# One TensorE-bound block kernel: rope, SiLU and softplus moved into the first projection, the delta rule's norms and turns into the local attention

## The reference, cut to what matters

```python
h = _rms_norm(x, g_mix_pre[l])
proj = h @ w_in[l]
aq, ak, av, dqkv, dgate, dalpha, dbeta = jnp.split(proj, IN_SPLITS, axis=-1)
aq = _rope(aq.reshape(b, s, ATTN_HEADS, ATTN_HEAD_DIM), positions)        # 8 heads of 64
ak = _rope(ak.reshape(b, s, ATTN_KV_HEADS, ATTN_HEAD_DIM), positions)     # 2 heads of 64
attn_o = _window_attention(aq, ak, av, attn_sink[l])                      # band of 128 each way
dn_o = _gated_deltanet(dqkv, dgate, dalpha, dbeta, conv_w[l], a_log[l], dt_bias[l], g_dn_out[l])
...
# in _gated_deltanet
conv = jax.nn.silu(conv.astype(jnp.float32))                              # 1536 channels, 5 taps
q = _l2norm(q) * (DN_HEAD_K ** -0.5)                                      # 4 heads of 128
k = _l2norm(k)
g = -jnp.exp(a_log) * jax.nn.softplus(a + dt_bias)
beta = jax.nn.sigmoid(bt)
# in each chunk, both directions
g = jnp.cumsum(g, axis=-1)
```

## Time and profile before

| what | value |
|---|---|
| median of 3 runs | 3808.03 us (3807.52 to 3812.46) |
| the profiled execution, first to last instruction (its span) | 3802.9 us |
| PE busy | 3621.9 us, 95% |
| DVE busy | 1925.5 us, 51% |
| ACT busy | 1436.0 us, 38% |
| `w_in` until the `rope_tables` barrier | to about 161 us |
| `rope_tables` and `rope` | about 161 to 184.8 us |
| `window` | 184.8 to 231.4 us |
| `delta_prep` | 231.4 to 267.2 us |

### The profile page before, as it was taken

How to read it: one execution, slowest core, us unless ns; L and a number is a source line. 1 busy time by engine, 2 the same in 40 slices (tenths; PEclk the granted TensorE clock), 3 DMA queues, 4 the chain that set the end, 5 groups by cost and what they waited for, 6 DMA issues and landing times.

```text
span 3802.9 us, 50067 instructions
## 1 busy us (share of the span) xinstructions
PE 3621.9 (95%) x19324; PEld 2946.7 (77%) x19324; DVE 1925.5 (51%) x3902; ACT 1436.0 (38%) x2538; POOL 107.4 (3%) x183
## 2 busy tenths in 40 slices
PE   7989989999999999999999989999899998889999
PEld 6779976788887888777777768888788886678887
DVE  5856746555455545555555544333433345764333
ACT  3251132432233222465556543223332234863222
POOL 0000001010001000000000000000000000000000
PEclk9999999999998999999999989999999999999999
DMA  6200036235543554211111212232223221012222
GB/s 243 95 1 1 1 128 226 89 121 176 187 147 125 192 177 146 81 67 51 51 51 50 73 54 89 89 111 89 90 83 117 72 75 45 2 45 89 87 91 78
DMA packets 47161, 359.77 MB, mean 95 GB/s; under 512 B 5217, under 2 KB 5601, under 8 KB 28129
## 3 DMA queue, kind: packets, MB, share of 16 engines
q1 hardware_dynamic: 23472, 269.31, 19.4%
q0 software_dynamic: 23472, 87.50, 6.9%
HBM read 354.69 MB, written 2.10 MB: 94 GB/s over the span
## 4 chain that ended last, share of the span: by engine, by line
PE 84%; DVE 8%; issue 3%; ACT 3%; DVEq 1%; DMA 0%; PEld 0%; ACTq 0%; PEldq 0%; POOL 0%; SPq 0%; POOLq 0%
PE bank L843 22%; PE bank L848 21%; PE bank L849 21%; PE bank L1679 5%; PE bank L2012 1%; PE bank L2029 1%; PE bank L2000 1%; PE bank L984 1%; PE bank L2485 1%; PE bank L2452 1%; DVE w_lo_sb L1280 1%; PE bank L1988 1%; PE bank L805 1%; PE bank L823 1%; PE bank L2474 1%
## 5 line engine op out<-in xcount | busy, mean ns | idle before, releaser
L843 PE MATMUL bank<-x_hi_sb,w_hi_sb 128*128 128x512 f32 x2936 | 1174.4, 400 | 59.6 <-DVE x_lo_sb L1422 15.7
L849 PE MATMUL bank<-x_hi_sb,w_lo_sb 128*128 128x512 f32 x2936 | 1151.4, 392 | 0.0
L848 PE MATMUL bank<-x_lo_sb,w_hi_sb 128*128 128x512 f32 x2936 | 1151.1, 392 | 0.0
L843 PEld LDWEIGHTS bank<-x_hi_sb,w_hi_sb 128*128 128x128 f32 x2936 | 555.5, 189 | 211.5 <-issue 66.1
L1103 ACT ACTIVATE w_hi_sb<-slab_sb 128x1024 fp32r<-128x1024 f32 (+2 forms) x555 | 507.1, 937 | 499.4 <-PE bank L843 312.0
L1280 DVE TENSOR_TENSOR w_lo_sb<-slab_sb,w_hi_sb 128x1024 fp32r<-128x1024 f32 (+2 forms) x555 | 580.8, 1078 | 187.4 <-ACT w_hi_sb L1103 172.2
L849 PEld LDWEIGHTS bank<-x_hi_sb,w_lo_sb 128*128 128x128 f32 x2936 | 555.0, 189 | 119.6
L848 PEld LDWEIGHTS bank<-x_lo_sb,w_hi_sb 128*128 128x128 f32 x2936 | 556.1, 189 | 109.2
L1446 DVE TENSOR_TENSOR hid_sb<-silu_gate_sb,bank 128x512 f32<-128x512 f32 x110 | 75.6, 687 | 602.1 <-PE bank L849 602.1
L843 PE MATMUL bank<-hid_hi_sb,w_hi_sb 128*128 128x512 f32 x880 | 342.8, 390 | 0.0
L849 PE MATMUL bank<-hid_hi_sb,w_lo_sb 128*128 128x512 f32 x880 | 342.6, 389 | 0.0
(11 more groups left out here) (361 smaller groups left out, 3742.4 us busy)
## 6 DMA issues: line engine op xcount, KB each, us to landing
slab_sb<-weights SPq DMA_DIRECT2D x79, 2048.0 KB, 7.9
keep_sb<-ada POOLq DMA_DIRECT2D x133, 512.0 KB, 4.5
slab_sb<-weights SPq DMA_DIRECT2D x44, 1536.0 KB, 6.5
slab_sb<-weights SPq DMA_DIRECT2D x20, 1280.0 KB, 6.0
tables_sb<-ada POOLq DMA_DIRECT2D x14, 512.0 KB, 6.2
work_sb<-ada POOLq DMA_DIRECT2D x13, 512.0 KB, 8.0
h_sb<-x SPq DMA_DIRECT2D x4, 512.0 KB, 6.7
out<-h_sb SPq DMA_DIRECT2D x8, 256.0 KB, 2.0
```

The costliest lines, as they stand in the source:

```text
L843: mm = pe.matmul(out, w_hi[p][:, w], hi, start=first, stop=False)
L848: pe.matmul(out, w_hi[p][:, w], lo, start=False, stop=False)
L849: return pe.matmul(out, w_lo[p][:, w], hi, start=False, stop=last)
```

## The change

Three barriers leave each engine's program, those that end `rope_tables`, `rope` and `delta_prep`. The one that ends `w_in` now stands behind the work of the first two, and the one that ends `window` behind that of the third.

- In `w_in`, the last slab is re-ordered so that the token-major part comes before the last two gate tiles. PE swaps tiles 0 and 1 after tile 18, tiles 2 and 3 after tile 19, tiles 4 and 5 after the token-major part. DVE ropes them in place. The angles are computed between weight parts in the first five steps; ACT takes the sines in step 7 and one SiLU tile per step from step 8 on. The softplus runs while PE is in the last tiles; PE makes the decay sums last.
- In `w_in`, 14 pieces of the modulation remain of 20. Six go to the first feed-forward layer: three pieces instead of two after each hidden tile of its first and last slabs.
- In `window`, `attend` calls a function `aside(i)` at the end of each iteration on each engine. PE: the sums of squares in i = 0 and 1, two spreads in each of i = 4 to 7, one tile's transposes in each of i = 3 and 8 to 14. ACT: four squares ahead of the loop, the roots in i = 2 with two table loads, copies of the transposes, three exponentials in i = 7. DVE: four squares and the decays ahead of the loop, the inversion in i = 3, two multiplications in each of i = 5 to 8.
- The dummy matmuls of `rope_tables`, `rope` and `delta_prep` go.

```diff
-ADA_TURNS = (20, 35, 105)
-ADA_EARLY = 52
+ADA_TURNS = (14, 35, 111)
+ADA_EARLY = 58
...
+                if aside is not None:
+                    aside(i)
...
+        def dve_rope_tile(e, j):
+            s = e.take(e.A, e.acc)
+            x, tmp = b1_qk[:, j, :], (b1_tmp[:, 3, :], b1_cv[0][:, 0:S])[j % 2]
+            dve.tensor_tensor(tmp, bank[s][:, :], b1_sin, ALU.mult).then_inc(e.A.free[s], 1)
+            e.link(dve.tensor_tensor(x, x, b1_cos, ALU.mult), dve_step)
+            dve.tensor_tensor(x, x, tmp, ALU.add)
...
+        DN_TILES = (4, 5, 6, 7, 0, 1, 2, 3)
+        DN_SPREADS = (4, 5, 6, 7)
+        DN_TURNS = (9, 10, 11, 12, 3, 8, 13, 14)
+        def pe_delta_ahead(e, i):
+            if i < 2:
+                if i == 0:
+                    e.norms = e.give(e.A, e.acc)
+                for j in DN_TILES[4 * i:4 * i + 4]:
+                    if j >= 4:
+                        pe.wait_ge(squared, e.nth(squared))
+                    else:
+                        pe.wait_ge(queries_squared, j + 1)
+                    for b in range(NB):
+                        at = j * NB + b
+                        mm = pe.matmul(e.A.bank[e.norms][:, at:at + 1], sq[:, j, b * P:(b + 1) * P], ones1, start=True,
+                                       stop=True)
...
+            if i in DN_SPREADS:
+                if i == DN_SPREADS[0]:
+                    pe.wait_ge(inverted, e.nth(inverted))
...
+            if i in DN_TURNS:
+                x = DN_TURNS.index(i)
+                if x < 4:
+                    pe.wait_ge(normed, e.nth(normed))
+                t = e.give(tp, e.tp)
+                for b in range(NB):
+                    mm = pe.transpose(turn_bank[t][:, b * P:(b + 1) * P], b1_qkv[:, 4 + x, b * P:(b + 1) * P], ident)
+                mm.then_inc(tp.full[t], 1)
+        def act_delta_ahead(e, i):
+            if i == 2:
+                act_root(e, 32, 1.0)
+                act_table(e, ACT.Exp)
...
             pe_parts_opening(e, x_hi, x_lo)
-            for _ in range(4):
+            for _ in range(3):
                 pe_parts(e, PARTS, KT, x_hi, x_lo, by_tile=True)
+            pe_parts(e, PARTS, KT, x_hi, x_lo, by_tile=True, between={2: swap(0), 3: swap(2)})
             e.slab.next()
+            pe_token_parts(e, 2, 2 * P, 2 * P)
+            pe_swap(e, b1_qk, 2, False, 4)
             for _ in range(2):
                 pe_tile_parts(e)
-            pe_token_parts(e, 2, 2 * P, 2 * P)
             pe_settle(e)
+            pe_decay_sums(e)
             e.stage_end("w_in")
-            pe_stay_busy(e, 40)
-            e.stage_end("rope_tables")
-            pe_swap(e, b1_qk, 6, wait=False)
-            pe_stay_busy(e, 20)
-            e.stage_end("rope")
-            attend(e, window_units(), 1, None)
+            attend(e, window_units(), 1, None, aside=lambda i: pe_delta_ahead(e, i))
...
+            dve_w_lo(e, 2, D)
+            dve.wait_ge(sines_ready, 1)
+            dve_rope_tile(e, 0)
+            dve_rope_tile(e, 1)
+            dve_w_lo(e, 3, D)
+            e.acc.pos += 1
+            dve_rope_tile(e, 2)
+            dve_rope_tile(e, 3)
+            dve_ada(e, 4)
             for b in range(NB):
                 s = e.take(e.A, e.acc)
                 dve.tensor_copy(b1_vtm[:, b, :], bank[s][:, 0:144]).then_inc(e.A.free[s], 1)
+            dve_decay_rates(e)
+            dve_rope_tile(e, 4)
+            dve_rope_tile(e, 5)
+            dve_decays(e)
+            dve_ada(e, 4)
...
                 if at in ("first", "mid", "last"):
-                    dve_ada(e, 2)
+                    dve_ada(e, 2 if at == "mid" else 3)
```

More of the change, by code:

```diff
@@ L540, in two_blocks @@
         b1_tmp = cut(work, 11848, 4, S)
-        b1_cos, b1_sin = b1_tmp[:, 0, :], b1_tmp[:, 1, :]
+        b1_cos, b1_sin = b1_tmp[:, 2, :], root_rows[:, :].bitcast(F32)
         P_SB = [cut(work, 11848 + 768 * i, 768) for i in range(3)]
-        PT = [cut(work, 14152 + 768 * i, 768) for i in range(2)]
+        PT = [cut(work, 768 * i, 768) for i in range(2)]
         m_col = [small[:, 160 + 24 * i:164 + 24 * i] for i in range(2)]
@@ L828, in pe_token_major, with pe_swap @@
                     between[b]()
-        def pe_swap(e, x, tiles, wait=True):
+        def pe_swap(e, x, tiles, wait=True, first=0):
             pe = e.eng
-            for j in range(tiles):
+            for j in range(first, first + tiles):
                 if wait:
@@ new lines, in dve_delta_squares @@
+        def dve_delta_squares(e):
+            dve = e.eng
+            for j in range(4):
+                dve.tensor_tensor(sq[:, j, :], b1_qkv[:, j, :], b1_qkv[:, j, :], ALU.mult).then_inc(queries_squared, 1)
+            e.tp.pos -= 1
+            t = e.take(tp, e.tp)
+            dve.tensor_copy(dn_s["G"], turn_bank[t][:, 0:32].rearrange("p (b x) -> p b x", b=NB))
+            e.link(dve.tensor_copy(dn_s["gl"], turn_bank[t][:, 32:64].rearrange("p (b x) -> p b x", b=NB)), dve_step)
+            dve.tensor_tensor(dn_s["diff"], dn_s["gl"], dn_s["G"], ALU.subtract).then_inc(dn["to_exp"], 1)
+            dve.drain().then_inc(tp.free[t], 1)
@@ new lines, in dve_delta_ahead @@
+        def dve_delta_ahead(e, i):
+            dve = e.eng
+            if i == 3:
+                dve_invert(e, 32, float(P) ** -0.5, 16)
+            if i - 1 in DN_SPREADS:
+                at = 2 * (i - 1 - DN_SPREADS[0])
+                for j in DN_TILES[at:at + 2]:
+                    s = e.take(e.S, e.sc)
+                    x = dve.tensor_tensor(b1_qkv[:, j, :], b1_qkv[:, j, :], e.S.bank[s][:, :], ALU.mult)
+                    x.then_inc(e.S.free[s], 1)
+                if j >= 4:
+                    dve.drain().then_inc(normed, 2)
+            if i == 9:
+                dve.wait_ge(dn["dec"], e.nth(dn["dec"]))
+                dve.tensor_tensor(dn_s["bG"], dn_s["beta"], dn_s["eG"], ALU.mult)
@@ L1656, in pe_delta @@
[L1656 to L1662, removed]
@@ L1820, in dve_delta @@
             dve.reciprocal(dn_s["beta"], dn_s["eb"])
[L1821 to L1835 removed]
+        def dve_delta(e):
+            dve = e.eng
+            tt = dve.tensor_tensor
+            for w in ways:
+                dve.memset(w.S, 0.0)
             full = [P, DH, P]
```

210 lines of the change are left out of this document (112 added, 98 removed).

## The result

The changed kernel takes **3788.5 us** (median of 4 runs, 3786.8 to 3789.9) against 3807.8 beside it: ratio 0.9945, 95% interval 0.9934 to 0.9957. That is 19.3 us faster. The forecast was 26.6 us, 3781, with a range of 3771 to 3796. The profiled execution took 3789.9 us, 1.9 over its span of 3788.0. Its span is 14.9 us under that of before. The missing 4 us lie in the executions: with 1.9 us around its span the profiled one of before took 3804.8, 3 us under its median, and the one here is 1.4 over its own. So the traces can explain 14.9 us, a little over half of the forecast.

The account below looks back on a forecast made before the run. PE, busy for 95% of the span, was taken to bound the kernel. Gains of 13.0 us (`w_in`) and 14.8 (35.8 of `delta_prep` less 21.0 window growth), less 1.2 (feed-forward), gave 26.6 us: 3781 us, range 3771 to 3796.

Parts of the forecast that it names:

- the 75 at which I would have called the account wrong: Stated sign of failure: the prediction is wrong if the window takes over 75 us; 67.7 was forecast.
- End of `w_in`: Last projection record to first score matmul: 24.4 us go, 11.4 us of PE work and waits replace them, 13.0 us gained.
- Head of the window: Window, i = 0 to 2: 64 records of sums at the low clock cost 11.6 us; i = 2 ends 8.9 us later.
- ACT's root: Window, i = 2 and 3: ACT's table load, root and load back take 3.1 us and PE waits; +3.8 us.
- Spreads, i = 4 to 7: Window: spreads add 1.83 us to each iteration, PE sets the pace at 4.1 instead of 2.45 us; +6.9 us.
- back at 1.00 by i = 4: Sign in the window: the clock is 0.50 over the sums and back at full by the fifth iteration.
- Turns: Window, i = 8 to 14: a transpose costs PE 0.46 and ACT 0.5 us; seven times 0.2, +1.4 us.
- First feed-forward layer: Second slab: PE's wait for DVE's weight part grows, as three modulation pieces precede it instead of two; 1.2 us lost.
- easy window: Rival: the window grows by only 12 us, as engines idle at its head and tail; 3772 us, chance 0.19.
- lockstep: Rival: each engine's new work stands where the next one waits; the window grows 35 us; 3795 us, chance 0.14.
- Low clock through the window: Rival: PE stays at 1.2 GHz through the window, about 105 us instead of 67.7; 3818 us, slower, chance 0.04.
- The loads of the modulation: Rival: 8.1 us reloads set the end of `w_in`, PE waits 2.4 us more before swap 4; 3788 us, chance 0.09.

Follow-up runs that it names:

- Run 6: Changed kernel with only VectorE's modulation pieces moved (three ahead of the value copies, two at the first feed-forward tile): median 3787.4 us, ratio 0.9943.
- run 2: Changed kernel with the squares and the 64 sums moved into the projection, a tile's sums between two projection tiles: median 3788.3 us, ratio 0.9939.
- run 3: As run 2, with the root and its inversion also moved into the projection stage: median 3774.9 us, ratio 0.9915.
- run 5: Changed kernel with the eight turns moved to units with four blocks and one behind the last: median 3787.5 us, ratio 0.9944.
- run 1: Changed kernel with squares, sums, root, spreads and turns done in one block behind the attention loop, not within it: median 3789.7 us, ratio 0.9954.
- run 11: The changed kernel once more, unedited, on the chip of run 9: median 3792.1 us, ratio 0.9949.
- run 4: As run 3, with VectorE's count of the score ring advanced by one, on the other chip: median 3780.8 us, ratio 0.9924.
- run 7: Run 4's kernel with 37 unused matmuls (8.5 us) added in the first feed-forward layer: median 3788.3 us, single runs 3778.4 to 3791.9.
- run 9: Changed kernel with sums, root and inversion in the projection, turns at four-block units, modulation pieces spread, decay sums at the stage's end: median 3771.7 us, ratio 0.9894.
- run 8: Changed kernel with sums, root and inversion in the projection, turns and modulation pieces moved, decay sums between the two gate tiles: median 3776.0 us, ratio 0.9911.

## Why the prediction held, point by point

The range held with room, and the change moved the time as forecast, but the parts that were off nearly all cost time. By the profiled executions the gain is 14.9 us of 26.6. The other 4.4 us of the measured 19.3 come from how the two profiled executions lie to their medians, which is luck. Without them the time would be 3793, still inside. One reading of mine was wrong as well: the 5.1 us "around the span" are 1.9 in every execution, and the rest is that the profiled one of before was 3 us faster than its median. The window took 74.4 us, just under the 75 at which I would have called the account wrong.

- **End of `w_in`**: forecast 13.0, measured 12.2. The modulation piece and its reload came out within 0.3 us. PE waited 1.35 instead of 2.1, and 0.57 instead of 0.8 in the token-major part; the decay sums with the gap behind them took 3.7 instead of 3.1, since the clock fell in them. About 1.2 us more are spread over the stage, and I did not take them apart. Run 6 shows the cause of the wait.
- **Head of the window**: the term of +8.9 was mis-sized; it measured +11.9. The step that failed is "11 records started in 2 us". A window's count takes in records that straddle its edges. By starts, 32 records took 6.91 us (175.56 to 182.47), 0.216 each and not 0.182, and the other 32 took 6.75: 13.7 and not 11.6 us, 2.1 of the 3.0. At the full clock the price is 0.101. The mechanism, sums at half clock, is what run 2 shows. The clock had fallen before them, though, in the decay sums, and stayed down through them.
- **ACT's root**: +3.8 forecast, +3.6 measured (28.3 - 22.3 = 6.0 us for i = 3, 2.4 before), and run 3 gets 3.4 back. The price of the earlier trace rows was right. By the Trainium skill ("ScalarE: Activation LUTs", "What ACT_TABLE_LOAD costs") it would have been an estimated 2.8 us more; this trace disagrees, with 1.29 us from a load to the next operation.
- **Spreads, i = 4 to 7**: +6.9 forecast, +7.8 measured (17.6 - 9.8). The first group of spreads ran in part at half clock, 2.44 us instead of 1.95: the clock fell once more behind PE's wait for the root, from 202.2 to 205.7, and was not "back at 1.00 by i = 4".
- **Turns**: +1.4 forecast, +4.4 measured. I had written of the unit with six blocks that fills both `turned` banks for i = 3, and did not carry it on to the turns at i = 9 to 14. Three waits, 3.2 us; run 5 takes them away, and 1.8 us of PE's idle time with them.
- **Recurrence**: it starts at full clock (1.16 us for eight records), a gain that I had not counted. It did not last: the clock fell at 263.7, and at 495 us the lead is 19.5.
- **First feed-forward layer**: 1.2 forecast, 4.02 - 2.88 = 1.14 measured, and run 6 gives it back. From 682 to 1189 the lead falls by 3.3 in all; 0.3 more is PE's wait at the slab before (2.55 us, 2.23 before), and the clock is at 0.50 from 792.8 to 796.2. The rest I did not take apart.
- **Sum**: at the recurrence 19.7 of 27.8. The 8.1 missing are 0.6 of a late start, 0.8 of `w_in` and 6.7 of the window (74.4 us, not 67.7).
- **Rivals**: "easy window" fell, with a growth of 27.7. That is half-way from the forecast's 21 to "lockstep" (35), and by run 1 the window hid nothing on balance. "Low clock through the window" did not come: a mean of 0.90 and 1.00 from i = 4 on. The Trainium skill ("TensorE: Matmul & The Clock Gate", "A second HAM failure mode: psum-queue depth-cycling") has small idles between groups make the clock swing; here the clock fell once from i = 4 on, behind the idle of 3.12 us, and from 205.7 to 247.5 it stayed at 1.00 through idles of 0.3 to 1.3 us. The loads of the modulation cost 1.35 us and not more.
- **Not in the forecast at all**: the clock's fall in the block near 2690 us. It took 6.3 of the lead in the profiled execution, and 8 in run 11's. Runs 3 and 4, with one order of work, show both cases in their profiles, and the times and mean clocks in runs 2, 7 and 9 fall apart in the same way. What decides it is open, and so is whether the changed kernel meets it always: both its profiles have it, and none of its nine times lies where one without it would.

## What to carry to other kernels

In this kernel a one-column matmul cost little among large ones and twice as much in a block of its own: put such sums between projection tiles, where they ran at 0.10 us a record and left the clock alone. Before you count on overlap, ask which engine the moved work runs on: where PE sets the pace already, its work adds one for one, and only the idle time around it can be won. When an edit of order moves a time by less than a late clock fall does (6 us here), judge it by the start of the next stage in the trace, which repeated within 2 us here where the medians of the same kernel differed by 3.6. And split even that into idle time and clock: of the 5 us that run 5 gained there, only 1.8 were waits.

## What the runs showed of the hardware

- Records of 128x1 took 0.101 us from start to start at the granted clock of 1.00 and 0.216 at 0.50, a little over double.
- The clock fell in dense blocks of narrow matmuls (24 decay sums of 4 and 8 columns in the changed kernel, 64 records of one column, 64 of 62 columns). It stayed at 1.00 with the same one-column records between 512-column ones, eight at a time (run 2), and with the same 24 decay sums between two gate tiles (run 8).
- Behind an idle of 1.75 us of PE in the projection it fell to 0.50 for 3.4 us in run 9 and stayed at 1.00 in run 3.
- Whether it falls in the block of 62 columns differed between runs 3 and 4, which have one order of work (on two chips), and between runs 4 and 7 on one chip. The fall takes 5 us in that block alone (12.3 against 7.3) and 6 to 8 with what follows.
